# Output projection of a decoder block: six of eight row tiles in pairs with seven block products

## The chip, the cores and the metric

One core of a Trainium2 chip runs the whole kernel. The metric is the device time of one execution in microseconds. Engines are named as in the profile: PE is TensorE, DVE VectorE, ACT ScalarE, POOL GpSimd, SP the engine whose queue issues most DMAs.

## The reference

A hybrid decoder block on x of 1024 tokens by 1024 channels (f32): adaLN-modulated norm, a projection, a gated linear attention branch and a differential attention branch, the gated merge of both, an output projection, and then a mixture of 32 experts of which each token takes two. What the change concerns:

```python
merged = (jax.nn.sigmoid(gate_a) * (o_a @ w_branch_a[l])
          + jax.nn.sigmoid(gate_b) * (o_b @ w_branch_b[l]))
x = x + gate1 * (merged @ w_out[l])
h2 = rms_norm(x, norm2_g[l]) * (1.0 + scale2) + shift2
y = hier_moe(h2, router_group_w[l], router_group_b[l], router_expert_w[l],
             router_expert_b[l], expert_w1[l], expert_w3[l], expert_w2[l])
x = x + gate2 * y
```

## The kernel before, in words

All matmuls are f32; each one of the code appears as two records in the trace. Nearly every matmul is issued through the helper `mm` (line 794), most of VectorE's additions and products through `tt` (line 1946), scalar_tensor_tensor through `stt` (line 1954), and ScalarE's work through `act` (line 1565). Engines are kept in step by counting semaphores, written out by hand; an engine's instructions run in the order in which they stand.

**Merge.** The merged activations are computed transposed into `mT`, 8 channel tiles by 1024 tokens, two channel tiles at a time. This stage already uses a scheme of seven block products for eight (`gate_products` and `branch_products` from line 1243, with VectorE's additions in `gate_adds`, `branch_adds`, `gate_branch_a` and `gate_branch_b`, lines 2441 to 2524). The last merge into `mT` raises `g_free` to 4 + 2 * KT.

**Output projection.** Eight row tiles of 128 tokens. Tile t needs, for each half of 512 output channels, 8 matmuls that accumulate over the channel tiles (`out_proj`, line 1314): stationary is a 128 x 128 piece of the tile that GpSimd has copied from `mT` into `ms` (`stage_merged`, line 687), moving is a piece of w_out of 512 columns. Tile 0 is taken straight from `mT` (lines 1307 to 1312), and its first 6 matmuls are issued ahead of the wait for the last merge. Even tiles write banks 0 and 1, odd tiles banks 2 and 3.

**What follows a tile.** VectorE multiplies each half by gate1 and adds x (`residual`, line 2568); ScalarE squares and sums it and takes the root; VectorE and ScalarE scale half of the row each (`normalised`, `x1_scaled`), and SP stores both forms (`store_x`, line 545). TensorE turns the tile by 8 transposes into banks 4 and 5 (`turn_x1`, line 1323), one VectorE copy (`turned`) and one ScalarE copy evict them, 8 small matmuls form the router's logits transposed (`route_apart`, line 1340), ScalarE reads them and one matmul turns them back (`turn_logits`). VectorE then chooses group and experts in a chain of 17 small dependent steps (`choose`, line 2597). The turning and routing of tile t - 1 is woven into the projection of tile t (`step`, line 1353). In VectorE's queue the order for tile t is: residual of half 0, eviction and choice of tile t - 1, residual of half 1, mean, scaling (lines 2645 to 2670).

**Tile 7.** Its projection is interleaved with the ranks of the tokens of tiles 0 to 5 (`fixed_ranks`, which waits for the choice of tile 5) and the first table of slots (`first_slots`), for which VectorE makes one-hot rows between the residuals (`filled_up`, `first_ids`, `first_onehot`, `first_table`). The last turn, of tile 7, waits for VectorE's last residual. After its routing the expert blocks begin.

**Loads.** SP's queue brings w_out after the last gate product (line 531), then expert weights into ten buffers of 2 MB, of which the buffers in R1, R3, R4, HT and WK come free as the stages end: the tile called (2, 1) behind w_out, (0, 1) and (1, 1) when the merge is done, and (0, 2), (1, 2), (2, 2) behind the stores of tiles 0, 1 and 2; (1, 0) and (0, 0) behind tile 7's two halves (lines 557 to 565). The first expert block uses (0, 1), (0, 2), (1, 1) and (1, 2). From then on each load waits for the block that used its buffer last (lines 582 to 592).

## Time and profile before

| | |
|---|---|
| median of 3 runs | 1479.59 us (1477.48 to 1481.29) |
| profiled execution | 1478.31 us |
| its span | 1476.4 us |
| busy PE / DVE / ACT / POOL | 1430.2 / 629.5 / 334.7 / 110.2 us |
| granted clock, mean | 0.992 |
| output projection | 810 to 940 us of the span |
| expert blocks | from 942 us to the end |

The profile is of one execution, with times from the start of its span. The granted clock is TensorE's, as a share of full speed. A row of a timeline gives start, duration, engine, line, operation, output <- inputs, shape and count of merged instructions; in brackets stands how long the engine was idle ahead of it and what released it. Durations of merged instructions run from the first start to the last end.

### The profile page before, as it was taken

What the parts mean: (1) busy time and instruction counts of PE and PEld (TensorE: products, weight loads), DVE (VectorE), ACT (ScalarE), POOL (GpSimd) and SP (SyncE); (2) the same over time, 40 slices, a digit from 0 to 9 for tenths busy, and PEclk for the clock granted to TensorE, in tenths of its full rate; (3) what the DMA queues carried; (4) which work ended last, traced back from release to release, by engine and by line L of the source; (5) the groups of instructions that cost most, each with busy time, mean ns of one, the idle gap of its engine ahead of it and who ended that gap; (6) DMA issues with size and microseconds to landing.
All of it is one profiled execution on the core that took longest, in us unless ns stands there. A gap on an engine that the chain in (4) does not pass through costs nothing.

```text
span 1476.4 us, 20298 instructions
## 1 busy us (share of the span) xinstructions
PE 1430.2 (97%) x8154; PEld 698.5 (47%) x8154; DVE 629.5 (43%) x1276; ACT 334.7 (23%) x673; POOL 110.2 (7%) x145
## 2 busy tenths in 40 slices
PE   7999999999999999999999999999989899999997
PEld 3544446888886565444444444443323233333332
DVE  4497444747465267554535545752110111111111
ACT  3513322232335453111111222311110111111110
POOL 2000000000000100000000001001121111111111
PEclk9999999999999999999999999999999999999999
DMA  9790200011112101112104752799999999999995
GB/s 357 256 368 1 66 0 1 29 29 29 29 29 58 29 1 43 43 29 57 29 29 171 299 213 85 259 367 404 414 410 409 403 374 394 407 415 404 405 413 168
DMA packets 80285, 292.55 MB, mean 198 GB/s; under 512 B 13408, under 2 KB 42302, under 8 KB 61505
## 3 DMA queue, kind: packets, MB, share of 16 engines
q1 hardware_dynamic: 73634, 274.51, 47.3%
q0 software_dynamic: 6560, 16.77, 4.5%
q8 instruction: 64, 1.05, 0.3%
q14 instruction: 27, 0.22, 0.0%
HBM read 277.47 MB, written 20.09 MB: 202 GB/s over the span
## 4 chain that ended last, share of the span: by engine, by line
PE 86%; DMA 5%; DVE 4%; SPq 3%; issue 1%; ACT 1%; POOL 0%; POOLq 0%; DVEq 0%; ACTq 0%
PE PS L794 81%; DMA R<-in_expert_w 4%; DVE R L1954 3%; SPq L378 2%; PE PS L1387 1%; PE PS L950 1%; PE PS L1470 1%; DMA R<-in_ada_w 0%; PE PS L1328 0%; PE PS L894 0%; DVE R L1946 0%; ACT R L1565 0%; DVE R L1950 0%; SPq L386 0%; PE PS L1162 0%
## 5 line engine op out<-in xcount | busy, mean ns | idle before, releaser
L794 PE MATMUL PS<-R 128*32 128x512 f32 (+4 forms) x3637 | 656.0, 570 | 20.4 <-DMA R<-in_ada_w 9.4
L794 PE MATMUL PS<-HT,R 128*32 128x512 f32 (+1 forms) x1576 | 423.6, 598 | 4.2 <-DMA R<-in_expert_w 4.2
L794 PEld LDWEIGHTS PS<-R 128*32 128x32 f32 (+2 forms) x3637 | 235.3, 127 | 325.8 <-issue 300.1
L794 PEld LDWEIGHTS PS<-HT,R 128*32 128x32 f32 (+1 forms) x1576 | 150.0, 138 | 195.1 <-issue 193.6
L794 PE MATMUL PS<-R,HT 128*128 128x512 f32 (+1 forms) x672 | 235.2, 506 | 2.6 <-ACT R L1565 1.5
L1946 DVE TENSOR_TENSOR R<-R,PS 128x512 f32<-128x512 f32 (+1 forms) x86 | 66.2, 780 | 343.0 <-PE PS L794 342.9
L1565 ACT ACTIVATE R<-PS 128x512 f32<-128x512 f32 (+3 forms) x116 | 69.6, 611 | 463.5 <-PE PS L794 302.4
L794 PEld LDWEIGHTS PS<-R,HT 128*128 128x128 f32 x672 | 125.8, 191 | 93.3 <-issue 82.0
L794 PE MATMUL PS<-WK,R 128*32 128x512 f32 (+1 forms) x440 | 98.0, 606 | 0.0
L1954 DVE SCALAR_TENSOR_TENSOR R<-PS,R,gate 128x1024 f32<-128x1024 f32 (+1 forms) x23 | 28.5, 1238 | 127.4 <-PE PS L794 127.4
L752 POOL DMA_INDIRECT out_rows<-R x36 | 52.3, 1453 | 298.8 <-DVE R L1954 158.5
L1946 DVE TENSOR_TENSOR R<-R 128x256 f32<-128x256 f32 (+11 forms) x109 | 65.7, 625 | 18.2 <-PE PS L794 16.3
L1565 ACT ACTIVATE R<-PS,att_nm 128x128 f32<-128x128 f32 (+7 forms) x64 | 46.8, 736 | 108.8 <-DVE att_nm L1950 108.8
L1565 ACT ACTIVATE R<-PS,S,A 128x128 f32<-128x128 f32 x92 | 34.4, 457 | 156.5 <-PE PS L1387 156.5
L794 PE MATMUL PS<-R,WK 128*128 128x128 f32 (+2 forms) x352 | 63.4, 324 | 2.1 <-DVE R L1950 1.6
L1565 ACT ACTIVATE WK<-PS 128x512 f32<-128x512 f32 (+8 forms) x56 | 34.1, 609 | 115.5 <-PE PS L950 48.7
L794 PEld LDWEIGHTS PS<-R,WK 128*128 128x128 f32 x352 | 46.8, 191 | 16.3 <-issue 16.1
L2165 DVE TENSOR_REDUCE att_mx<-PS 128x2 f32<-128x256 f32 (+7 forms) x32 | 43.3, 1354 | 20.6 <-PE PS L794 20.4
L1565 ACT ACTIVATE WK<-R 128x128 f32<-128x128 f32 (+2 forms) x56 | 34.2, 611 | 77.3 <-DVE R L1946 73.9
L1954 DVE SCALAR_TENSOR_TENSOR R<-R,cact 128x2048 f32<-128x2048 f32 (+1 forms) x23 | 46.6, 2026 | 3.0 <-DMA R<-in_ada_w 1.2
L794 PE MATMUL PS<-R,gate 128*128 128x256 f32 (+1 forms) x224 | 47.1, 366 | 0.0
L794 PEld LDWEIGHTS PS<-R,gate 128*128 128x128 f32 x224 | 39.5, 190 | 6.4 <-issue 1.7
(275 smaller groups left out, 935.2 us busy)
## 6 DMA issues: line engine op xcount, KB each, us to landing
R<-in_expert_w SPq DMA_DIRECT2D x38, 2048.0 KB, 22.9
R<-in_expert_w SPq DMA_DIRECT2D x48, 1024.0 KB, 13.0
HT<-in_expert_w SPq DMA_DIRECT2D x15, 2048.0 KB, 26.9
R<-in_ada_w SPq DMA_DIRECT2D x16, 1024.0 KB, 5.0
HT<-in_expert_w SPq DMA_DIRECT2D x16, 1024.0 KB, 13.2
WK<-in_expert_w SPq DMA_DIRECT2D x7, 2048.0 KB, 25.4
R<-in_w_in SPq DMA_DIRECT2D x24, 512.0 KB, 4.1
R<-in_ada_w SPq DMA_DIRECT2D x16, 512.0 KB, 10.7
```

What stands on the lines that cost most here:

```text
L378: e.dma_start(dst, src, allow_slow_non_contiguous=True).then_inc(s[loaded], 16)
L752: e.indirect_dma_start(out, bass.IndirectOffsetOnAxis(idx, 0), rows_out, None, compute_op=ALU.add, bounds_check=T - 1, oob_is_err=False).t ...
L794: return nc.tensor.matmul(o, l, r, start=a, stop=z)
L950: last = nc.tensor.transpose(bank(4 + j // 4)[:, (j % 4) * P:(j % 4 + 1) * P], attn[i % 2][:, j * P:(j + 1) * P], ident[:, :])
L1387: last = nc.tensor.transpose(bank(j // 4)[:, (j % 4) * P:(j % 4 + 1) * P], xg[u][:, j * P:(j + 1) * P], ident[:, :])
L1470: last = nc.tensor.transpose(bank(4)[:, j * P:(j + 1) * P], hh[:, j * P:(j + 1) * P], ident[:, :])
L1565: return nc.scalar.activation(o, i, f, **kw)
L1946: return v.tensor_tensor(o, a, b, op)
L1954: return v.scalar_tensor_tensor(out=o, in0=a, scalar=c, in1=b, op0=op0, op1=op1)
L2165: att(v.tensor_reduce(att_mx[:, i % 2, :], score_v[:, :, 0:(i + 1) * P], AX.X, ALU.max))
```

## The change

Tiles 0 to 5 are projected as three pairs of 256 tokens. A pair's rows, the 1024 channels in between and the 1024 output channels are each halved, and the two by two blocks are multiplied with seven block products (each four matmuls) instead of eight:

- GpSimd makes sums and differences: of w_out once (`ot1`, `ot2`, `ot4`, 2048 elements a partition each; `ot3` is made by VectorE within the last merge step), and of each pair's activations (`os1` to `os4`, 512 elements each, `pair_sums`). It copies only tiles 6 and 7 as before.
- TensorE runs `pair_steps`: seven products into banks 0, 2, 1, 3, 0, 1, 2. All of it stands behind the wait for the last merge. Between the products of pair q the turning and routing of both tiles of pair q - 1 is placed; that of tiles 4 and 5 goes into tile 6. The logits of odd tiles use bank 7.
- ScalarE copies the first product into SBUF (`pair_first`), VectorE makes seven additions a pair (early, middle, late) with the tiles in `pair_c`, then both tiles' residuals from SBUF (`pair_residual`), then their scaling and evictions. Choices of pair q - 1 stand between the additions of pair q, those of tiles 4 and 5 behind pair 2: tile 4 ahead of the residual of tile 6, tile 5 between its halves.
- Three expert weight tiles that were loaded during the projection are issued behind the pairs, since their buffers now hold the sums.

The diff without waits that only count on and without renamed counts:

```diff
+        ob11, ob12, ob21, ob22 = (wout_h[n][:, k:k + 4, :] for k in (0, 4) for n in range(2))
+        ot1, ot2, ot3, ot4 = (x.rearrange("p (k n) -> p k n", k=4) for x in
+                              (R1[:, 4096:6144], R3[:, 0:2048], R1[:, 6144:8192], R3[:, 3072:5120]))
+        os1, os2, os3, os4 = (R4[:, 6144 + 512 * i:6656 + 512 * i].rearrange("p (k t) -> p k t", k=4) for i in range(4))
+        pair_c = [sig[:, x, :] for x in range(4)]
+        NPAIR = 3
...
-            load_ew(2, 1, FIXED[1])
...
-                if t < 3:
-                    load_ew(t, 2, FIXED[2])
+                if t == 0:
+                    load_ew(2, 2, FIXED[2])
+                if t == 3:
+                    e.wait_ge(s["mo_mm"], 7 * NPAIR)
+                    load_ew(2, 1, FIXED[1])
+                if t == 4:
+                    e.wait_ge(s["x1_ready"], 4 * NPAIR)
+                    load_ew(1, 2, FIXED[2])
+                if t == 5:
+                    e.wait_ge(s["mo_mm"], 7 * NPAIR + 2)
+                    load_ew(0, 2, FIXED[2])
             store_x(NT - 2, 0)
-            e.wait_ge(s["mo_mm"], 2 * NT - 1)
+            e.wait_ge(s["mo_mm"], 7 * NPAIR + 3)
             load_ew(1, 0, FIXED[0])
-            e.wait_ge(s["mo_mm"], 2 * NT)
+            e.wait_ge(s["mo_mm"], 7 * NPAIR + 4)
...
+            def pair_sums(q):
+                a11, a12, a21, a22 = token_pair(q)
+                if q > 0:
+                    e.wait_ge(s["mo_mm"], 7 * q - 5)
+                e.tensor_tensor(os3, a11, a21, ALU.subtract).then_inc(s["st_s"], 1)
+                if q > 0:
+                    e.wait_ge(s["mo_mm"], 7 * q - 3)
+                e.tensor_tensor(os1, a21, a22, ALU.add).then_inc(s["st_s"], 1)
+                e.wait_ge(s["st_s"], 50 + 4 * q)
+                e.tensor_tensor(os2, os1, a11, ALU.subtract).then_inc(s["st_s"], 1)
+                e.wait_ge(s["st_s"], 51 + 4 * q)
+                if q > 0:
+                    e.wait_ge(s["mo_mm"], 7 * q)
+                e.tensor_tensor(os4, a12, os2, ALU.subtract).then_inc(s["st_s"], 1)
+
+            e.wait_ge(s["in_ld9"], 48)
+            e.wait_ge(s["st_t"], 13)
+            e.tensor_tensor(ot1, ob12, ob11, ALU.subtract).then_inc(s["st_t"], 1)
+            e.wait_ge(s["st_t"], 14)
+            e.tensor_tensor(ot2, ob22, ot1, ALU.subtract).then_inc(s["st_t"], 1)
             e.wait_ge(s["g_free"], 4 + 2 * KT)
-            stage_merged(1, 1)
-            with e.Fori(1, NT // 2) as i:
-                for u in range(2):
-                    wait_apart(e, (s["mo_mm"], 2 * (2 * i + u) - 2))
-                    stage_merged(2 * i + u, u)
-
-
-            e.wait_ge(s["ms_ready"], NT - 1)
+            pair_sums(0)
+            e.wait_ge(s["st_t"], 15)
+            e.tensor_tensor(ot4, ob21, ot2, ALU.subtract).then_inc(s["st_t"], 1)
+            stage_merged(NT - 2, 0)
+            for q in range(1, NPAIR):
+                pair_sums(q)
+            e.wait_ge(s["mo_mm"], 7 * NPAIR)
+            stage_merged(NT - 1, 1)
...
-            for half in range(2):
-                for k in range(KT):
-                    if half == 0 and k == KT - 2:
-                        e.wait_ge(s["g_free"], 4 + 2 * KT)
-                    last = mm(bank(half), mT[:, k, 0:P], wout[half][k], k == 0, k == KT - 1)
-                last.then_inc(s["mo_mm"], 1)
+            e.wait_ge(s["g_free"], 4 + 2 * KT)
...
+            def pair_product(b, x, w):
+                for k in range(4):
+                    ins = mm(bank(b), x[:, k, :], w[:, k, :], k == 0, k == 3)
+                ins.then_inc(s["mo_mm"], 1)
...
+            def pair_steps(q):
+                a11, a12, a21, a22 = token_pair(q)
+                added, sums = ADDED_MERGE + 7 * q, 48 + 4 * q
+                if q > 0:
+                    e.wait_ge(s["st_u"], added - 2)
+                pair_product(0, a11, ob11)
+                yield
+                if q > 0:
+                    e.wait_ge(s["st_u"], added)
+                e.wait_ge(s["st_s"], sums + 1)
+                pair_product(2, os3, ot3)
+                yield
+                e.wait_ge(s["st_t"], 15)
+                e.wait_ge(s["st_s"], sums + 3)
+                pair_product(1, os2, ot2)
+                yield
+                pair_product(3, os1, ot1)
+                yield
+                e.wait_ge(s["st_m1"], 13 + q)
+                pair_product(0, a12, ob21)
+                yield
+                e.wait_ge(s["st_t"], 16)
+                e.wait_ge(s["st_u"], added + 1)
+                pair_product(1, a22, ot4)
+                yield
+                e.wait_ge(s["st_s"], sums + 4)
+                e.wait_ge(s["st_u"], added + 2)
+                pair_product(2, os4, ob22)
...
+            def turn_both(t):
+                turn_x1(t, t % 2, 0)
+                turn_x1(t, t % 2, 1)
 
             e.wait_ge(s["small_ld"], 16 * (N_SMALL + 2))
-            with e.Fori(0, NT // 2 - 1) as i:
-                for u in (1, 0):
-                    step(2 * i + 2 - u, u)
-                    out_proj(2 * i + 2 - u, u, 1, 2, 4)
-                    turn_logits(2 * i + 1 - u)
-                    out_proj(2 * i + 2 - u, u, 1, 4, KT)
+            for q in range(NPAIR):
+                product_of_pair = pair_steps(q)
+                next(product_of_pair)
+                if q > 0:
+                    turn_both(2 * q - 2)
+                next(product_of_pair)
+                if q > 0:
+                    turn_both(2 * q - 1)
+                    route_apart(2 * q - 2, 0)
+                next(product_of_pair)
+                if q > 0:
+                    turn_logits(2 * q - 2)
+                    route_apart(2 * q - 1, 1)
+                next(product_of_pair)
+                if q > 0:
+                    turn_logits(2 * q - 1)
+                for _ in range(3):
+                    next(product_of_pair)
+            out_proj(NT - 2, 0, 0, 0, 4)
+            turn_both(NT - 4)
+            out_proj(NT - 2, 0, 0, 4, KT)
+            turn_both(NT - 3)
+            route_apart(NT - 4, 0)
+            out_proj(NT - 2, 0, 1, 0, 4)
+            turn_logits(NT - 4)
+            route_apart(NT - 3, 1)
+            out_proj(NT - 2, 0, 1, 4, KT)
+            turn_logits(NT - 3)
...
+            def pair_first(q):
+                e.wait_ge(s["mo_mm"], 7 * q + 1)
+                e.wait_ge(s["g_free"], 4 + 2 * KT)
+                e.wait_ge(s["x1_ready"], 4 * q)
+                act(pair_c[0], bank(0), ACT.Copy).then_inc(s["st_m1"], 1)
+
+            pair_first(0)
+            for q in range(NPAIR):
+                for u in range(2):
+                    t = 2 * q + u
+                    for half in range(2):
+                        x1_square(t, u, half)
+                    x1_root(t, u)
+                    if u == 0:
+                        x1_turned(t, u)
+                x1_scaled(2 * q, 0)
+                x1_turned(2 * q + 1, 1)
+                x1_scaled(2 * q + 1, 1)
+                if q + 1 < NPAIR:
+                    pair_first(q + 1)
+                logits_read(2 * q)
+                logits_read(2 * q + 1)
...
+                if p == KT // 2 - 2:
+                    e.wait_ge(s["in_ld9"], 48)
+                    tt(ot3, ob22, ob12, ALU.subtract).then_inc(s["st_t"], 1)
...
+            def pair_adds_early(q):
+                c11, c12, c21, c22 = pair_c
+                added = ADDED_MERGE + 7 * q
+                e.wait_ge(s["st_m1"], 13 + q)
+                e.wait_ge(s["mo_mm"], 7 * q + 3)
+                e.wait_ge(s["x1_ready"], 4 * q)
+                tt(c12, c11, bank(1), ALU.add).then_inc(s["st_u"], 1)
+                e.wait_ge(s["st_u"], added + 1)
+                tt(c21, c12, bank(2), ALU.add).then_inc(s["st_u"], 1)
+
+            def pair_adds_middle(q):
+                c11, c12, c21, c22 = pair_c
+                added = ADDED_MERGE + 7 * q
+                e.wait_ge(s["st_u"], added + 2)
+                e.wait_ge(s["mo_mm"], 7 * q + 4)
+                tt(c22, c21, bank(3), ALU.add).then_inc(s["st_u"], 1)
+                tt(c12, c12, bank(3), ALU.add).then_inc(s["st_u"], 1)
+
+            def pair_adds_late(q):
+                c11, c12, c21, c22 = pair_c
+                added = ADDED_MERGE + 7 * q
+                e.wait_ge(s["mo_mm"], 7 * q + 5)
+                tt(c11, c11, bank(0), ALU.add).then_inc(s["st_u"], 1)
+                e.wait_ge(s["st_u"], added + 4)
+                e.wait_ge(s["mo_mm"], 7 * q + 6)
+                tt(c21, c21, bank(1), ALU.add).then_inc(s["st_u"], 1)
+                e.wait_ge(s["mo_mm"], 7 * q + 7)
+                tt(c12, c12, bank(2), ALU.add).then_inc(s["st_u"], 1)
+                e.wait_ge(s["st_u"], added + 7)
+
+            def pair_residual(q, u):
+                t = 2 * q + u
+                for half in range(2):
+                    x, c = slice(half * 512, (half + 1) * 512), pair_c[2 * u + half]
+                    if half == 0:
+                        e.wait_ge(xn_st[u], 16 * (t // 2 + 1))
+                        e.wait_ge(s["mods_ld"], 16 * 6)
+                    tt(c, c, gate[:, 0, x], ALU.mult).then_inc(s["mo_gated"], 1)
+                    e.wait_ge(s["mo_gated"], 2 * t + half + 5)
+                    e.wait_ge(xh_ld[u], 16 * (t // 2 + 1))
+                    tt(xh[u][:, x], xh[u][:, x], c, ALU.add).then_inc(s["x1_ready"], 1)
+                mean_square(t)
...
+            def tail_begin(q):
+                pair_residual(q, 0)
+                pair_residual(q, 1)
+                normalised(2 * q)
+                turned(2 * q)
+                e.wait_ge(s["xn2_ready"], 4 * q + 2)
+                normalised(2 * q + 1)
+                turned(2 * q + 1)
+
+            pair_adds_early(0)
+            pair_adds_middle(0)
+            pair_adds_late(0)
+            for q in range(1, NPAIR):
+                tail_begin(q - 1)
+                if q == 1:
+                    rt(v.memset(prior_b[:, 0, :], 0.0))
+                pair_adds_early(q)
+                choose(2 * q - 2)
+                pair_adds_middle(q)
+                choose(2 * q - 1)
+                pair_adds_late(q)
+            tail_begin(NPAIR - 1)
+            choose(NT - 4)
+
+            for t in (NT - 2, NT - 1):
...
```

## Rows read from the trace of the kernel before

**Rows 1.** The chain that ended last, from the page: shares of the span by engine.

```profile
PE 86%; DMA 5%; DVE 4%; SPq 3%; issue 1%; ACT 1%; POOL 0%; POOLq 0%; DVEq 0%; ACTq 0%
```

**Rows 2.** Stretches of 6 us: PE, PEld, DVE, ACT, POOL busy, granted clock, DMA share, GB/s.

```profile
804.00:810.00 6.00, 6.00 (x15) 2.65 (x14) 3.48 (x6) 0.00 (x0) 0.00 (x0) 1.00 0.00 1
...
924.00:930.00 6.00, 6.00 (x27) 3.34 (x28) 4.73 (x14) 2.45 (x4) 0.00 (x0) 1.00 0.54 178
...
964.00:970.00 6.00, 6.00 (x60) 1.82 (x56) 5.31 (x21) 0.60 (x1) 0.00 (x0) 1.00 0.58 199
...
976.00:982.00 6.00, 4.80 (x44) 3.60 (x48) 4.56 (x10) 1.50 (x4) 0.00 (x0) 1.00 1.01 421
```

**Rows 3.** Timeline of PE in the expert stage: the longest waits for weights.

```profile
1107.29 1.07 PE L794 MATMUL PS<-R 128*32 128x512 f32 x2 [3.95 <-DMA WK<-in_expert_w]
...
1112.38 0.69 PE L794 MATMUL PS<-R 128*32 128x512 f32 x2
...
1170.03 0.63 PE L794 MATMUL PS<-HT,R 128*32 128x512 f32 x3 [4.17 <-DMA R<-in_expert_w]
```

**Rows 4.** Timeline of PE in the output projection: turns of tiles and the last turn.

```profile
810.25 20.80 PE L794 MATMUL PS<-HT,R 128*128 128x512 f32 x48
...
830.88 1.04 PE L1328 MATMUL PS<-ident,R 128*128 128x128 f32 x8
...
846.92 1.04 PE L1328 MATMUL PS<-ident,R 128*128 128x128 f32 x8
...
847.79 1.88 PE L794 MATMUL PS<-HT,R 128*128 128x512 f32 x4
...
911.05 1.04 PE L1328 MATMUL PS<-ident,R 128*128 128x128 f32 x8
...
939.29 0.66 PE L1328 MATMUL PS<-ident,R 128*128 128x128 f32 x4 [0.38 <-DVE R L1946]
...
941.81 3.62 PE L794 MATMUL PS<-R 128*32 128x512 f32 x16
```

**Rows 5.** Timeline of DVE, tiles 5 to 7: sixth choice, residuals, its one wait.

```profile
916.91 0.25 DVE L1954 SCALAR_TENSOR_TENSOR small_w<-PS,stat,rbias 128x36 f32<-128x36 f32 x1 [3.64 <-PE PS L794]
...
921.18 0.69 DVE L1946 TENSOR_TENSOR WK<-PS,gate 128x512 f32<-128x512 f32 x1
...
922.51 0.15 DVE L1951 TENSOR_SCALAR stat<-stat 128x1 f32<-128x1 f32 x1
...
927.87 0.69 DVE L1946 TENSOR_TENSOR WK<-PS,gate 128x512 f32<-128x512 f32 x1 [0.94 <-PE PS L794]
```

**Rows 6.** Timeline of DVE at the end of the merge.

```profile
800.11 0.69 DVE L1946 TENSOR_TENSOR R<-R,WK 128x512 f32<-128x512 f32 x1
...
809.52 0.69 DVE L1946 TENSOR_TENSOR gate<-gate,WK 128x512 f32<-128x512 f32 x1
...
814.59 0.69 DVE L1946 TENSOR_TENSOR R<-R 128x512 f32<-128x512 f32 x1
```

**Rows 7.** Instructions by line and form: GpSimd's and VectorE's elementwise rows.

```profile
L644 POOL TENSOR_TENSOR tri<-tri,blk 64x128 f32<-64x128 f32 x1 | 0.4, 447 | 0.1
...
L683 POOL COPY WK<-R 128x512 f32 x4 | 2.5, 613 | 34.9 <-PE PS L794 34.9
...
L688 POOL COPY R<-R 128x1024 f32 x6 | 6.3, 1045 | 83.0 <-PE PS L794 83.0
...
L1946 DVE TENSOR_TENSOR R<-R 128x1024 f32<-128x1024 f32 x20 | 24.2, 1222 | 16.5 <-PE PS L794 16.3
```

**Rows 8.** Timelines: a small VectorE addition beside a GpSimd copy, and alone.

```profile
840.44 1.04 POOL L688 COPY R<-R 128x1024 f32 x1 [14.97 <-PE PS L794]
...
840.48 1.02 DVE L1946 TENSOR_TENSOR R<-R 128x32 bf16<-128x32 bf16 x1
...
904.54 0.17 DVE L1946 TENSOR_TENSOR R<-R 128x32 bf16<-128x32 bf16 x1
```

**Rows 9.** Stretch of 2 us behind the last wait for weights, columns as in rows 2.

```profile
1172.00:1174.00 2.00, 2.00 (x16) 0.78 (x12) 0.00 (x0) 0.00 (x0) 0.00 (x0) 0.51 0.97 363
```

More of the change, by code:

```diff
@@ L331, in build, with mean_no, root_no @@
         wout = [[w[:, k, :] for k in range(KT)] for w in wout_h]
+        ob11, ob12, ob21, ob22 = (wout_h[n][:, k:k + 4, :] for k in (0, 4) for n in range(2))
[4 more added lines that the diff above has]
+        NPAIR = 3
+        def mean_no(t):
+            return 2 * t + 1 - (t % 2 if t < 2 * NPAIR else 0)
+        def root_no(t):
+            return 2 * t + 2 + (1 - t % 2 if t < 2 * NPAIR else 0)
+        ADDED_MERGE = 28 * (KT // 2 - 1)
+        ADDED_PAIRS = ADDED_MERGE + 7 * NPAIR
         xh = [R4[:, 4096 + 1024 * i:5120 + 1024 * i] for i in range(2)]
-        ms = [R4[:, 6144 + 1024 * i:7168 + 1024 * i].rearrange("p (k t) -> p k t", k=KT) for i in range(2)]
+        ms = [x.rearrange("p (k t) -> p k t", k=KT) for x in (R3[:, 2048:3072], R4[:, 6144:7168])]
         xn = [WK[:, 1024 * i:1024 * (i + 1)] for i in range(2)]
@@ L1316, in out_proj @@
                     if half == 0:
-                        e.wait_ge(s["ms_ready"], t)
-                    e.wait_ge(s["mo_gated"], 2 * t + half + 1)
+                        e.wait_ge(s["ms_ready"], u + 1)
+                    e.wait_ge(s["st_u"], ADDED_PAIRS - 2 + half if u == 0 else ADDED_PAIRS)
                 for k in range(k0, k1):
@@ L1340, in route_apart @@
             def route_apart(t, u):
-                e.wait_ge(s["rt_done"], t + 1)
+                e.wait_ge(s["rt_done"], max(t, 1))
                 for k in (0, 4, 1, 5, 2, 6, 3, 7):
@@ L1345, in route_apart @@
                     r = 64 * (k // 4)
-                    last = mm(bank(6)[r:r + NR, 64:64 + P], wr[:, k, :], h2T[u][:, k, :], k % 4 == 0, k % 4 == 3)
+                    last = mm(bank(6 + u)[r:r + NR, 64:64 + P], wr[:, k, :], h2T[u][:, k, :], k % 4 == 0, k % 4 == 3)
                 last.then_inc(s["rt_pr"], 1)
@@ L1869, in logits_read @@
                 for r in (0, 64):
-                    last = act(logits_t[r:r + NR, :], bank(6)[r:r + NR, 64:64 + P], ACT.Copy)
+                    last = act(logits_t[r:r + NR, :], bank(6 + t % 2)[r:r + NR, 64:64 + P], ACT.Copy)
                 last.then_inc(s["rt_lg"], 1)
-            for half in range(2):
-                x1_square(0, 0, half)
-            x1_norm(0, 0)
-            with e.Fori(0, NT // 2 - 1) as i:
-                for u in (1, 0):
-                    t = 2 * i + 2 - u
-                    x1_turned(t - 1, 1 - u)
-                    x1_square(t, u, 0)
-                    logits_read(t - 1)
-                    x1_square(t, u, 1)
-                    x1_norm(t, u)
+            def pair_first(q):
[19 more added lines that the diff above has]
+                logits_read(2 * q + 1)
+            for half in range(2):
+                x1_square(NT - 2, 0, half)
+            x1_norm(NT - 2, 0)
             x1_turned(NT - 2, 0)
@@ L2570, in residual @@
                 c = slice(half * 512, (half + 1) * 512)
-                e.wait_ge(s["mo_mm"], 2 * t + half + 1)
+                e.wait_ge(s["mo_mm"], 7 * NPAIR + 2 * (t - NT + 2) + half + 1)
                 if half == 0:
@@ L2600, in choose @@
                 c = slice(t, t + 1)
-                stt(logits[:, t, :], bank(6)[:, 0:NR], stat[:, 2, t % 2:t % 2 + 1], rbias[:, :], ALU.mult, ALU.add).then_inc(s["rt_done"], 1)
+                stt(logits[:, t, :], bank(6 + t % 2 if t < 2 * NPAIR else 6)[:, 0:NR], stat[:, 2, t % 2:t % 2 + 1], rbias[:, :], ALU.mult, ALU.add).then_inc(s["rt_done"], 1)
                 e.wait_ge(s["rt_done"], t + 2)
@@ L2643, in first_table @@
                 stt(tab_tok[:, c], pad, -1.0, a, ALU.add, ALU.add).then_inc(s["tab_done"], 1)
-            for t in range(NT):
+            def tail_begin(q):
[21 more added lines that the diff above has]
+            for t in (NT - 2, NT - 1):
                 if t == NT - 1:
```

39 lines of the change are left out of this document (18 added, 21 removed).

## The prediction

> **What bounds the kernel now.** I read the page's chain of waits first [rows 1]. The reader is to see that TensorE holds 86% of the chain that ends last and VectorE 4%. Then I read the stretches of 6 us. From 976 us on the transfers run at 421 GB/s with the 16 DMA engines full [rows 2], and TensorE stands for weights there, the longest times for 3.95 and 4.17 us [rows 3]. Every load of that stretch waits for a buffer that TensorE has finished with, and from 964 to 970 us, ahead of the saturation, the transfers still have room (0.58 busy, [rows 2]) because no buffer is free. So the expert stage hangs on the moment at which TensorE enters it. I take a shift of that entry to reach the end one for one.
>
> In the stage that is changed, TensorE has no gap: the last branch product gives way to row tile 0 at 810.25, and the turns of tiles come every 16.03 us (831 and 847, [rows 4]). VectorE waits for TensorE in every tile. That holds up to the last tile: from the start of the sixth choice at 916.91 to the last residual VectorE stands only 0.94 us [rows 5], and TensorE waits for that residual at 939.29 [rows 4]. The entry at 941.8 thus follows the end of VectorE's queue.
>
> **What is saved.** From 810.25 to 830.88 TensorE works off 48 records [rows 4], 0.43 us each; two records are one matmul, 0.858 us, so a product of four takes 3.43. A pair needs 28 of them where two tiles needed 32: 3.43 us less, 10.3 us for three pairs.
>
> **The start.** Before, 6 matmuls (5.15 us) of tile 0 run ahead of the last merge, which ends at 815.28 [rows 6]. Afterwards TensorE waits for that merge with nothing to do, from 810.25. That cover of 5.0 us is lost whatever else happens.
>
> VectorE gets one subtraction of 2048 elements a partition. No row has this form; 1024 elements take 1.22 us [rows 7] and 512 take 0.69 [rows 6], so 2.3 us, from 800.75 to 803.05. Between there and 809.52 stand six branch additions of 0.69 that wait for TensorE's products, 1.72 us apart, so 2.3 us of the wait are used up and the queue catches up. I cost it at nothing. The transfers are idle from 804 [rows 2], with an expert tile of 5 us behind w_out, so w_out is there by 799; without this cover up to 2.3 us would fall on the merge.
>
> GpSimd then makes the first two weight differences, 2048 elements each, ahead of the merge. The one tensor_tensor it has is 447 ns for 128 elements [rows 7]. Copies of 512 and 1024 take 0.61 and 1.045 us, about 0.2 us and 0.84 ns an element. With that fixed part the tensor_tensor costs 2.1 ns an element: 4.5 us for 2048, 1.25 us for 512. The lower bound is the copy's rate, 1.9 us for 2048; the upper is a smaller fixed part, 4.8 us. I take 4.5, since that row is the same operation. They run 803.1 to 807.6 and 807.6 to 812.1.
>
> VectorE's products and merges from 809.52 on read SBUF twice. The rows show what that means: an addition of 32 columns takes 0.17 us alone and 1.02 us when it meets a GpSimd copy, and both end together, at 841.5 [rows 8]. So the operation of 809.52 starts at 812.1: 2.6 us. The Trainium skill (SBUF — State Buffer, Who interferes with whom) says that such a VectorE instruction and a GpSimd one that reads SBUF exclude each other for a whole instruction. By that rule the long differences block as I charge them; if a hold were never longer than the copies show, the start would cost 1.6 us less. The bounds of this term are 0 (differences at the copy's rate, over by 807) and 3.2 us. The merge ends at 817.9, and TensorE has been idle for 7.7 us.
>
> After idle times of 3.95 and 4.17 us the granted clock fell to 0.5 (0.51 from 1172 to 1174), the lower level of 1.2 GHz, and matmuls of 0.6 us took 1.07 [rows 3, 9]. It was low from 1107.3 to about 1112.4 and from about 1170.5 to 1173.8, and half of that is lost: 2.6 and 1.7 us. I take 2.1 us for the restart; the bounds are 0 and, for the longer idle time, twice the smaller, 3.4.
>
> Pair 0 has no turns between its products: 817.9 + 24.0 + 2.1 = **844.0** for its end. GpSimd's four sums (5 us) and the last difference (4.5 us) end 9.7 us into it; its products need them from 3.4 and from 17 us on, so they cost nothing. Were my rate for them half as much again, they would still be in time.
>
> **Pairs 1 and 2.** A tile's routing work costs 16.03 - 13.73 = 2.3 us of TensorE, 4.6 a pair. New are waits at each border between pairs. After a pair's last product VectorE has one addition left (0.69) and then eight operations of 0.69 at 0.60 to 0.72 apart, where before it had two after a half tile. GpSimd's fourth sum is released at the same instant and blocks the first of them until 1.6 us after the border. The second half of tile 2q is ready 4.35 us after it; TensorE, with one product and four turns, is there at 3.87. Half a microsecond. The first tile's eviction from the shared turn bank stands behind the second tile's residual, at 9.2 us; TensorE asks at 8.7. Another half. Bounds 0 and 3 us a pair; I take 1.1. A pair thus lasts 24.0 + 4.6 + 1.1 = 29.7 us. Additions, choices and late additions of VectorE fit in it: the choice takes 4.3 us undisturbed [rows 5] and the sums on GpSimd add 1 to 2 us. Pair 2 ends at 844.0 + 59.4 = **903.4**. Before, tile 6 starts at 911.05 - 6.87 = 904.2 [rows 4]. TensorE is level.
>
> **The tail.** At this point the old order had one tile left to turn and route; the new one has two, and their choices stand one behind the other in VectorE's queue with one half's residual between. Before, the sixth choice starts 12.7 us after tile 6 (916.91). Now the fifth starts there, plus one turn (0.87, [rows 4]) and the border's 1.1: 14.7 us. It takes 4.3, the residual 1.3 (921.18 to 922.51, [rows 5]), and the sixth choice starts at 903.4 + 20.3 = 923.7. From there the queue is the old one, less the 0.94 us that it stood: 923.7 - 916.9 - 0.9 = **5.9 us later**. TensorE waits for it at the ranks, the first slots and the last turn. The bounds here: 0 if the choices were hidden by TensorE, 2 us more if GpSimd's constants block them.
>
> **The loads.** Three expert tiles (2 MB, some 5 us each at 400 GB/s) leave SP's queue at 788, 835 and 848 us and come behind the pairs; the fourth moves from the third tile's store to the first's. Behind the pairs the engines are 0.54 busy or less, as from 924 to 930 [rows 2]; 6 MB fit, and they are issued by 922, more than 20 us ahead of the first block. The queue entries behind them (x of tiles 6 and 7) are needed over 8 us after they can land. Nothing, with 3 us as the upper bound.
>
> **Sum.** Up to the end of pair 2: -10.3 (products) + 5.0 (cover) + 2.6 (blocked VectorE) + 2.1 (clock) + 2.2 (two borders) = +1.6 us, and one routing of 2.3 us fewer has been done by then than at the start of tile 6 before: -0.7, which is the 903.4 against 904.2. The tail then adds 6.7: **+5.9 us**. The profiled execution took 1478.31 us (span 1476.4), which gives 1484.2; the median of the runs stands 1.3 us above it, and I give **1485.5**.
>
> **Rivals.**
> 1. *VectorE's tail is hidden* (not slower). Then TensorE's own count decides: tile 6 with two routings and a border takes 13.7 + 4.6 + 1.1 = 19.4 us, and tile 7 starts at 922.8 where it started at 904.2 + 16.0 = 920.2: +2.6 us, 1482, within what can be told. For it speaks that VectorE waits in each tile now; against it that its queue is already full behind tile 5. It decides if the sixth choice starts by 920.4, 2.6 us after its old time and the 0.9 us of standing. Chance 0.17.
> 2. *The start is cheap*: differences at the copy's rate, no block, and a restart at full clock. 4.7 us less, +1.2: 1481. Chance 0.12.
> 3. *The weight stream takes up the delay*: if the loads didn't move with TensorE, the 8.1 us of the two waits and 4.3 us of low clock [rows 3] would shrink, and the end would come at 1472 to 1480. Against it: the engines are not full before 970 us. Chance 0.11.
> 4. *VectorE and GpSimd block each other in every choice*, also in the tail: 3 us a pair, 2 us behind, 1490 to 1494. Chance 0.10.
> That the products don't fall to seven is excluded by the code. My forecast has 0.50.
>
> **Numbers.** A measurement tells 0.3% (4.4 us) from no change. Faster by more needs rival 3 nearly whole: 0.08. Within 0.3%: rivals 1 and 2, part of 3, and the lower third of my own case: 0.40. Slower: 0.52. The range runs from rival 2 and the upper part of 3 to the lower end of rival 4: 1478.5 to 1491.
>
> **What would show it.** TensorE idle 7 to 8 us ahead of the first pair product, with two GpSimd tensor_tensor of 4.5 us and a VectorE product ending late beside the second; a stretch at 0.5 behind it; borders with two waits of half a microsecond; the end of pair 2 at 903; the sixth choice at 923.7; the last turn at 945. It is wrong if TensorE reaches that turn without a wait, if GpSimd takes 2 us, or if the weight waits shrink.

## The result and the profile after

The changed kernel takes 1486.03 us (median of 5 runs, 1485.38 to 1487.08), the kernel before 1479.59 (5 runs): a ratio of 1.0047, 95% interval 1.0036 to 1.0059. It is slower by 0.5%, and 1485.5 had been predicted.

The profiled execution took 1487.06 us, its span is 1485.2. Already a GpSimd fill at 492.25 us stands 2.59 us later than before (489.66), where the two programs are the same. I take this shift, and its like in every trace below, off and call what is left local. The start times in the rows are as the profile has them. The last turn came at 939.29 [rows 4] and comes at 948.36: 9.07 later, 6.5 us local. The spans differ by 8.8 - 2.6 = 6.2.

TensorE around pair 0 of the changed kernel (timeline: start, duration, engine, line, operation, count, idle time ahead and its releaser):

```profile
802.54 10.46 PE L841 MATMUL PS<-R 128*128 128x512 f32 x24
820.72 5.61 PE L841 MATMUL PS<-HT,R 128*128 128x512 f32 x8 [7.71 <-DVE R L2060]
826.16 10.46 PE L841 MATMUL PS<-R 128*128 128x512 f32 x24
836.47 3.60 PE L841 MATMUL PS<-HT,R 128*128 128x512 f32 x8
839.90 3.60 PE L841 MATMUL PS<-R 128*128 128x512 f32 x8
843.33 7.03 PE L841 MATMUL PS<-HT,R 128*128 128x512 f32 x16
850.20 0.60 PE L1408 MATMUL PS<-ident,R 128*128 128x128 f32 x4
```

Before, this engine had no gap here [rows 4]. The first product behind the gap takes 5.61 us where a later one takes 3.60; the granted clock is 0.50 from 820 to 824 us and 1.00 from 826 us on. The 16 records at 843.33 are pair 0's last product and pair 1's first, so pair 0 ends at 846.77. GpSimd and VectorE meanwhile (two timelines, of POOL and of DVE):

```profile
805.75 4.52 POOL L733 TENSOR_TENSOR R<-HT 128x2048 f32<-128x2048 f32 x1 [251.01 <-DVE R L2060]
810.35 4.50 POOL L735 TENSOR_TENSOR R<-HT,R 128x2048 f32<-128x2048 f32 x1
...
820.54 1.27 POOL L720 TENSOR_TENSOR R<-R 128x512 f32<-128x512 f32 x1 [5.68 <-DVE R L2060]
```

```profile
811.39 0.69 DVE L2060 TENSOR_TENSOR WK<-WK,PS 128x512 f32<-128x512 f32 x1 [1.10 <-PE PS L841]
812.12 3.28 DVE L2060 TENSOR_TENSOR gate<-gate,WK 128x512 f32<-128x512 f32 x1
815.33 0.68 DVE L2060 TENSOR_TENSOR R<-R,WK 128x512 f32<-128x512 f32 x1
...
819.77 0.69 DVE L2060 TENSOR_TENSOR R<-R 128x512 f32<-128x512 f32 x1
```

The product at 812.12 takes 3.28 us where its like take 0.69. It lies beside the second difference and ends at 815.40, just behind the end of that one at 814.85. The last merge, at 819.77, is 2.6 us late for it. The tail of the stage, TensorE first, then GpSimd, then VectorE:

```profile
908.94 1.25 PE L1408 MATMUL PS<-ident,R 128*128 128x128 f32 x8
915.34 0.63 PE L1408 MATMUL PS<-ident,R 128*128 128x128 f32 x4 [1.28 <-DVE WK L2742]
930.23 0.55 PE L841 MATMUL PS<-R 128*128 128x24 bf16 x6 [1.20 <-DVEq L2774]
936.35 0.31 PE L841 MATMUL PS<-R 128*128 128x2 bf16 x6 [1.06 <-DVE R L2060]
947.45 1.06 PE L1487 MATMUL PS<-ident,R 128*128 128x128 f32 x8 [1.59 <-DVE WK L2060]
948.36 0.60 PE L1408 MATMUL PS<-ident,R 128*128 128x128 f32 x4
```

```profile
939.90 2.02 POOL L784 DMA_INDIRECT R<-xn_rows,R  x1 [25.69 <-DMA xn_rows<-WK]
```

```profile
938.32 0.55 DVE L2068 SCALAR_TENSOR_TENSOR R<-R 128x1 f32<-128x1 f32 x3
```

TensorE stands four times, 5.1 us, where it stood 0.4 [rows 4]. The last of these stands is ahead of the transposes of the gathered rows (L1487), which the first expert block needs. The indirect DMA that fetches those rows (the gather) starts at 939.90. The bracket of its row names a store, but the gather waits only for the stores of tiles 0 to 5, of which the last, issued at 917.37, landed 12.0 us later, and for VectorE's first table, which is done at 938.87. The gather starts 1.0 us behind the table, as it did before (930.54 and 931.53). TensorE takes up its rows at 947.45, 7.5 us behind its start; before, it had landed after 5.5 us.

Behind the entry, the waits for weights did not shrink, which settles the rival of the stream that takes up a delay (summary of TensorE's waits from 960 us on: total, times, longest; after, then before):

```profile
PE PS L841 <- DMA R<-in_expert_w: 8.8, 3, 4.1
PE PS L841 <- DMA WK<-in_expert_w: 4.0, 1, 4.0
```

```profile
PE PS L794 <- DMA R<-in_expert_w: 7.8, 3, 4.2
PE PS L794 <- DMA WK<-in_expert_w: 4.0, 1, 4.0
```

### The profile page after: what moved, and what is told of

It is laid out like the page before. It is cut to its first block and busy times, and to the rows that moved or that the text cites. A ratio compares the mean times of both kernels' runs of the same rounds, so it can differ in the third digit from the quotient of the medians.

```text
span 1485.2 us, 20233 instructions
## 1 busy us (share of the span) xinstructions
PE 1423.6 (96%) x8130; PEld 696.1 (47%) x8130; DVE 651.4 (44%) x1298; ACT 334.4 (23%) x676; POOL 136.5 (9%) x155
## 5 line engine op out<-in xcount | busy, mean ns | idle before, releaser
L841 PE MATMUL PS<-R 128*32 128x512 f32 (+5 forms) x3733 | 697.0, 568 | 24.7 <-DMA R<-in_ada_w 9.6
L841 PEld LDWEIGHTS PS<-R 128*32 128x32 f32 (+3 forms) x3733 | 252.5, 128 | 349.0 <-issue 318.4
L841 PE MATMUL PS<-HT,R 128*32 128x512 f32 (+1 forms) x1456 | 373.0, 601 | 11.9 <-DVE R L2060 7.7
L2060 DVE TENSOR_TENSOR R<-R,PS 128x512 f32<-128x512 f32 x107 | 80.2, 762 | 366.4 <-PE PS L841 362.7
L841 PEld LDWEIGHTS PS<-HT,R 128*32 128x32 f32 (+1 forms) x1456 | 128.8, 135 | 181.6 <-issue 180.7
L2060 DVE TENSOR_TENSOR R<-R 128x512 f32<-128x512 f32 (+11 forms) x121 | 73.2, 625 | 18.6 <-PE PS L841 16.3
## 6 DMA issues: line engine op xcount, KB each, us to landing
R<-in_expert_w SPq DMA_DIRECT2D x48, 1024.0 KB, 12.5
```

What stands on the lines that cost most here:

```text
L841: return nc.tensor.matmul(o, l, r, start=a, stop=z)
L2060: return v.tensor_tensor(o, a, b, op)
```

## Experiments

The measured ratios are to runs of the kernel before on the same chip. In us a ratio is multiplied by its 1480. The changed kernel was not run again beside them; its 1.0047 is that of the result. Each interval reaches 1.3 to 2.2 us to either side, so a step of 1 or 2 us rests on its one trace.

**Start, cover alone: the kernel before, with TensorE's tile 0 behind the last merge.**

```diff
             e.wait_ge(s["g_sig"], 4 * (KT - 2))
+            e.wait_ge(s["g_free"], 4 + 2 * KT)
             for half in range(2):
```

> The kernel before, with one wait added: TensorE's row tile 0 stands until the last merge, as the pairs do. Nothing else is changed. Theory (the cover is worth 5.0 us and the shift reaches the end one for one, with about 1.5 us more of low clock behind an idle time of 5 us): every turn of a row tile comes 5.0 to 7.0 us later, the entry to the experts too, the end at 1479.6 + 6.5 = 1486. Rival 1 (the weight stream takes up the delay): entry 6 us later, end less than 2 us later, the waits for weights shorter. Rival 2 (VectorE's queue of the last tiles has slack that swallows it): entry less than 3 us later.

Measured: 1486.87 us, ratio 1.0046 (1.0032 to 1.0061), 6.8 us. TensorE's timeline, and the two stretches behind the wait (PE, PEld, DVE, ACT, POOL busy, granted clock, DMA share, GB/s):

```profile
818.22 22.91 PE L794 MATMUL PS<-HT,R 128*128 128x512 f32 x48 [5.01 <-DVE R L1947]
...
949.37 0.66 PE L1329 MATMUL PS<-ident,R 128*128 128x128 f32 x4 [0.37 <-DVE R L1947]
```

```profile
818.00:822.00 4.00, 3.78 (x5) 1.74 (x6) 1.35 (x4) 0.00 (x0) 1.04 (x1) 0.50 0.71 208
822.00:826.00 4.00, 4.00 (x10) 1.68 (x10) 0.61 (x4) 0.00 (x0) 0.00 (x0) 0.95 1.04 398
```

The 48 records took 20.80 us [rows 4] and take 22.91, 2.1 us more, at a clock of 0.50 at first. With the 5.01 us of idle time this is 7.1, and the last turn comes 10.08 - 2.79 = 7.3 us late (local), with the same wait ahead of it. Cover and restart (the low clock behind an idle time) together reach the end one for one. Both rivals fall.

**Start, block alone: GpSimd's second difference behind the merge.**

```diff
-            e.wait_ge(s["st_t"], 14)
-            e.tensor_tensor(ot2, ob22, ot1, ALU.subtract).then_inc(s["st_t"], 1)
...
                 e.tensor_tensor(os3, a11, a21, ALU.subtract).then_inc(s["st_s"], 1)
+                if q == 0:
+                    e.wait_ge(s["st_t"], 14)
+                    e.tensor_tensor(ot2, ob22, ot1, ALU.subtract).then_inc(s["st_t"], 1)
```

> The changed kernel with GpSimd's second weight difference (4.5 us) placed behind the last merge and the first sum instead of ahead of it, where it lay beside a VectorE product that ended 2.6 us late. Theory (VectorE and GpSimd hold each other off): that product takes 0.69 us instead of 3.28, the last merge ends 2.6 us earlier and pair 0 starts 2.6 us earlier; the idle time is 5.1 us. The three sums behind the difference come 4.5 us later, but 6 us into a pair of 24, with the products that need them from 3.4 to 17 us on: up to 2 us of wait at the third or fourth product. Time 1483.4 without that wait, 1485.4 with it. Rival (VectorE's product ended late because TensorE's products or ScalarE's reads came late, and the difference only lay beside it): the merge ends where it did, 1486 or later.

Measured: 1483.04 us, ratio 1.0021 (1.0011 to 1.0030). The same product on VectorE, then TensorE's first product:

```profile
808.99 0.69 DVE L2061 TENSOR_TENSOR gate<-gate,WK 128x512 f32<-128x512 f32 x1
```

```profile
814.99 5.12 PE L842 MATMUL PS<-HT,R 128*128 128x512 f32 x8 [5.12 <-DVE R L2061]
```

Without the difference beside it the product takes 0.69 us and TensorE's idle time falls by 2.59. No later product of pair 0 waits. The last turn comes 3.2 us earlier than in the changed kernel (local). The difference beside the product was the cause of its length.

**Start, clock alone: 8 idle matmuls.**

```diff
             e.wait_ge(s["g_sig"], 4 * (KT - 2))
+            for _ in range(8):
+                mm(bank(5), ident[:, :], wout[0][0])
             e.wait_ge(s["g_free"], 4 + 2 * KT)
```

> The changed kernel with 8 more matmuls of 128 x 128 by 512, whose result nobody reads, in TensorE's 7.7 us of idle time ahead of pair 0. Nothing starts earlier; only the idle time is filled. Theory (the restart at the low clock costs 2.0 us): no stretch at 0.50 behind the wait, the second and third pair products at 0.43 us a record from their start, pair 0 ends 2.0 us earlier, 1484.0, a ratio of 1.0033. Rival (the low stretch costs nothing that reaches the end, because GpSimd's sums or VectorE would hold pair 0 anyway): pair 0 ends where it did, 1486.

Measured: 1484.37 us, ratio 1.0024 (1.0015 to 1.0033). TensorE:

```profile
812.94 7.03 PE L841 MATMUL PS<-HT,ident 128*128 128x512 f32 x16
820.62 3.70 PE L841 MATMUL PS<-HT,R 128*128 128x512 f32 x8 [0.65 <-DVE R L2062]
```

The first product takes 3.70 us and not 5.61, the granted clock stays at 1.00, and pair 0 ends 2.1 us earlier (local), of which 0.2 us are an earlier start. The last turn gains 1.6: half a us is lost again at the gathered rows, where TensorE now stands 2.1 us. The runs differ from the changed kernel's by more, 3.4 us; the trace does not show the rest.

**Start, products moved ahead of the merge.** The first product of pair 0, then the first two with GpSimd's sum for the second. The cut below is TensorE's part of the second edit; GpSimd's waits ahead of its sums move in the same way. In the first edit the second product keeps the wait for the merge.

```diff
-            e.wait_ge(s["g_free"], 4 + 2 * KT)
+            e.wait_ge(s["g_free"], 2 * KT)
...
+                if q == 0:
+                    e.wait_ge(s["g_free"], 4 + 2 * KT)
```

> The changed kernel, with the first pair product of pair 0 let ahead of the wait for the last merge: it reads only channel tiles 0 to 3, which are there. Theory (the loss is the cover of the last merge, each us of TensorE's start reaches the end one for one): TensorE's 7.7 us of idle time become 4.3, the end comes 3.4 us earlier than in the changed kernel, 1482.6 on the scale of its median of 1486.0, a ratio of 1.0023 to the kernel before instead of 1.0047. The low clock behind the wait stays, since 4.3 us are about as long as the waits of 3.95 and 4.17 us that it followed before. Rival 1 (the end hangs on VectorE's queue of the last tiles, not on TensorE's start): the start moves by 3.4 us and the last turn by less than 1. Rival 2 (the clock's restart is tied to the long idle time): it goes too, 5.4 us earlier, 1480.6.

> The changed kernel, with the first two pair products of pair 0 ahead of the wait for the last merge, and GpSimd's sum for the second of them made as soon as its channel tiles are there. Theory: 6.9 us of the 7.7 us of idle time are filled, the granted clock doesn't fall, so 6.9 + 2.0 = 8.9 us less than the changed kernel: 1477.1, a ratio of 0.9985 to the kernel before. GpSimd's sum of 1.26 us ahead of ot1 may push its queue and VectorE's last merge back by up to 1.3 us: 1478.4 at worst. Rival 1 (VectorE's queue of the last tiles sets the end): less than 2 us gained, 1484 or more. Rival 2 (the clock costs nothing): 1479.

Measured: 1483.46 us, ratio 1.0017 (1.0008 to 1.0027), and 1483.26, 1.0019 (1.0010 to 1.0027). The first comes out near its time, but with 5.51 us of idle time where 4.3 were expected, and its last turn is only 2.3 us earlier (local). The second was a miss. TensorE in the two:

```profile
822.21 12.13 PE L841 MATMUL PS<-R 128*128 128x512 f32 x24 [5.51 <-POOL R L720]
```

```profile
823.68 8.80 PE L845 MATMUL PS<-R 128*128 128x512 f32 x16 [4.02 <-POOL R L729]
```

Each product moved ahead brings the next one to GpSimd's sums, of which two, 1.26 us each, can only follow the last merge. In my sum they cost nothing; that held only while a product without sums stood ahead of them. The clock fell behind the idle 4.02 us too (0.53 from 826 to 828 us).

**Loads alone, in the kernel before: first with the waits of the changed kernel.**

```diff
-            load_ew(2, 1, FIXED[1])
...
-                if t < 3:
-                    load_ew(t, 2, FIXED[2])
+                if t == 0:
+                    load_ew(2, 2, FIXED[2])
+                if t == 3:
+                    e.wait_ge(s["mo_mm"], 12)
+                    load_ew(2, 1, FIXED[1])
+                if t == 4:
+                    e.wait_ge(s["x1_ready"], 12)
+                    load_ew(1, 2, FIXED[2])
+                if t == 5:
+                    e.wait_ge(s["mo_mm"], 14)
+                    load_ew(0, 2, FIXED[2])
```

> The kernel before, with three loads of expert weights (2 MB each) moved behind the row tiles 5 and 6, where the changed kernel has them. Theory: nothing, 1479.6 within 1 us, the waits for weights of 3.95 and 4.17 us and the entry at 941.8 as they were. Rival (the later loads push the weight stream back, and part of the changed kernel's loss is theirs): up to 3 us later, with longer waits for weights from 1100 us on.

Measured: 1487.01 us, ratio 1.0046 (1.0034 to 1.0058). This does not tell what the loads cost. TensorE stands in a new place, for VectorE, which waits for a store:

```profile
921.03 1.92 PE L802 MATMUL PS<-WK,wr 128*36 128x128 f32 x14 [5.33 <-DVE WK L2590]
```

```profile
917.58 0.69 DVE L1954 TENSOR_TENSOR WK<-PS,gate 128x512 f32<-128x512 f32 x1 [6.72 <-DMA xn_rows<-WK]
```

My wait for the end of tile 5, put behind x of tile 5, held the store of tile 4 in SP's queue (at 906.78 us where it stood at 891.10 before). In the changed kernel SP stands 12.5 us for the same event, but there the next store is due only at 909.50 us. So once more, with no wait added:

```diff
-            load_ew(2, 1, FIXED[1])
...
-                if t < 3:
-                    load_ew(t, 2, FIXED[2])
+                if t == 0:
+                    load_ew(2, 2, FIXED[2])
+                if t == 5:
+                    load_ew(2, 1, FIXED[1])
+                    load_ew(1, 2, FIXED[2])
             store_x(NT - 2, 0)
+            load_ew(0, 2, FIXED[2])
```

> The kernel before, with the same three loads of expert weights (2 MB each) moved back, but without a wait of their own: two stand behind the request for x of tile 7 (some 912 us), one behind the stores of tile 6 (some 925 us). In the experiment before, they stood behind waits that also held the stores of tiles 4 and 5 and the request for x of tile 6; its 7.8 us may be those waits' and not the loads'. Theory: the loads cost nothing, 1479.3 within 1.5 us, a ratio of 1.000, the entry to the experts where it was, no wait of TensorE ahead of tile 6. Rival (the loads themselves cost: they keep the transfers of x and the stores of tiles 6 and 7 back, or the weights of the experts): 3 to 8 us more, with the last residuals waiting for transfers.

Measured: 1482.96 us, ratio 1.0029 (1.0014 to 1.0043). TensorE at the gathered rows; then loads, stores and the gather among the issues between 925 and 950 us (KB each, us to landing), first in this kernel, where no landing of the gather is recorded, then in the one before:

```profile
943.68 1.06 PE L1390 MATMUL PS<-ident,R 128*128 128x128 f32 x8 [2.21 <-issue]
```

```profile
HT<-in_expert_w SPq DMA_DIRECT2D x4, 1024.0 KB, 10.3
xn_rows<-WK SPq DMA_DIRECT2D x2, 512.0 KB, 6.1
```

```profile
HT<-in_expert_w SPq DMA_DIRECT2D x4, 1024.0 KB, 6.1
xn_rows<-WK SPq DMA_DIRECT2D x2, 512.0 KB, 4.9
R<-xn_rows,R POOLq DMA_INDIRECT x1, 5.5
```

From 925 to 950 us packets take 99% of the DMA engines' time, before 78%. The gather starts where it did (934.98 - 3.43 = 931.55, before 931.53), so no store holds it. It is not there when TensorE asks at 941.47: its rows are used 8.7 us behind its start, where it had landed after 5.5. The last turn comes 5.29 - 3.43 = 1.9 us late (local). The runs give 4.3 us, with an interval from 2.1; what lies above 1.9 the trace does not show.

**Tail: two pairs in place of three.**

```diff
-        NPAIR = 3
+        NPAIR = 2
```

(and tiles 5 and 6 taken back into the old order on all engines)

> The changed kernel with two pairs in place of three: row tiles 0 to 3 in pairs, 4 to 7 in the old way. Theory (the third pair saves 3.43 us, but makes VectorE's queue of the last tiles 6.7 us late, and with tiles 5 to 7 one by one VectorE catches up before tile 7): 6.7 - 3.43 - 1.1 for a border, with up to 1 us of the tail left: 2.5 to 4.4 us less than the changed kernel, 1482 to 1483.5, a ratio of 1.002. VectorE stands in tile 6 again, and the last residual is waited for by less than 1 us. Rival (the tail isn't late because of the third pair; the loss is all at the start): 3.4 us more than the changed kernel less a border of 1, 1488.

Measured: 1485.84 us, ratio 1.0043 (1.0031 to 1.0055), the last turn 0.2 us earlier (local). A miss, and of arithmetic: TensorE's own work is longer by 3.43 us, which the sum had left out, and of the 5.1 us of waits 1.7 stay. The third pair saves what it costs.

> Two pairs in place of three, and the first two products of pair 0 ahead of the wait for the last merge. Theory (the two losses are apart and add): 8.9 + 3.5 us less than the changed kernel, 1473.6, a ratio of 0.996 to the kernel before, faster than both. Rival (one slack is shared, so that after the first gain the second is worth nothing): 1477.

The edit is the two before, together. Measured: 1482.23 us, ratio 1.0019 (1.0010 to 1.0029), as with three pairs. Neither the theory nor the rival had it, since both counted on the 8.9 us at the start.

**The start filled.** The first two products run ahead of the merge as above. VectorE makes the two sums that follow the merge, GpSimd the second difference behind it, and the product that reads it comes fifth. VectorE's part:

```diff
+            e.wait_ge(s["g_free"], 4 + 2 * KT)
+            tt(os1, v21, v22, ALU.add).then_inc(s["st_s"], 1)
+            e.wait_ge(s["st_s"], 50)
+            tt(os2, os1, v11, ALU.subtract).then_inc(s["st_s"], 1)
```

> The changed kernel with all of TensorE's 7.7 us of idle time filled: the first two products of pair 0 run ahead of the wait for the last merge; VectorE makes the two sums that need the last merge (0.7 us each in place of 1.26 on GpSimd, behind each other); GpSimd makes the second weight difference behind the merge, and the product that reads it comes fifth in pair 0 and not third. The moved first two products alone gave 3.6 us and not 8.9, because TensorE then stood 4.0 us for GpSimd's sums and the clock still fell. Theory: TensorE stands for less than 1 us ahead of pair 0's third product, the granted clock stays at 1.00, the entry to the experts comes 9 us earlier than in the changed kernel: 1477, a ratio of 0.998 to the kernel before. Rival (VectorE's queue or GpSimd's differences of 4.5 us now hold a later product of pair 0): 2 to 4 us of it come back, 1480.

> The same with two pairs in place of three. Two pairs alone gave 0.2 us in the trace, because TensorE's own count is 3.43 us longer and only the 5 us of waits on VectorE in the last tiles go. Theory (the third pair saves what it costs, whatever the start): the same as with three pairs within 1 us, 1477. Rival (with the start filled, the end of VectorE's queue matters more, and two pairs win): 2 to 3 us less than with three.

Measured: 1478.27 us, ratio 0.9991 (0.9980 to 1.0002), and with two pairs 1478.06, 0.9991 (0.9982 to 1.0001). The gap ahead of pair 0 is gone, and inside the pair 3.7 us have come back, as the rival had it: 1.93 of a wait and 1.8 of low clock. GpSimd, VectorE and TensorE of the version with three pairs:

```profile
825.77 4.51 POOL L743 TENSOR_TENSOR R<-HT,R 128x2048 f32<-128x2048 f32 x1
```

```profile
826.50 4.79 DVE L2700 COPY suf<-ident 36x36 f32<-36x36 f32 x2
831.33 3.33 DVE L2072 TENSOR_TENSOR R<-R,PS 128x512 f32<-128x512 f32 x5
```

```profile
832.16 5.37 PE L845 MATMUL PS<-R 128*128 128x512 f32 x8 [1.93 <-DVE R L2072]
```

The two small copies of 36 columns stand beside the difference for 4.79 us, the additions stand behind it, and TensorE behind them; the product takes 5.37 us and not 3.6, at a low clock again (0.57 from 832 to 834 us). With two pairs the wait is there too, 1.92 us, but the clock stays at 1.00.

**The last two differences on VectorE too** (two pairs).

```diff
+            e.wait_ge(s["st_t"], 14)
+            tt(ot2, ob22, ot1, ALU.subtract).then_inc(s["st_t"], 1)
+            e.wait_ge(s["st_t"], 15)
+            tt(ot4, ob21, ot2, ALU.subtract).then_inc(s["st_t"], 1)
```

> Two pairs, the start filled as in the runs before, and GpSimd's last two weight differences (2048 elements each) made by VectorE instead, right behind the last merge. In the trace of the run before, GpSimd's last difference held a VectorE copy for 4.8 us, VectorE's first additions of the pair stood behind it, and TensorE stood 1.9 us for them in the middle of pair 0. Theory: VectorE makes both differences in 4.6 us while nothing else is due on it, TensorE has no wait over 0.7 us in pair 0 and the clock stays at 1.00: 1.9 us less than with GpSimd, 1476.5, a ratio of 0.998 to the kernel before, an interval that leaves 1 out. Rival (VectorE's additions now stand behind its own differences, or the stream of expert weights takes up the gain): 1478, as before.

Measured: 1477.07 us, ratio 0.9981 (0.9972 to 0.9990): faster than the kernel before by 0.2%, and than the changed one. Against the version with GpSimd's differences (0.9982 to 1.0001) the intervals overlap; in the traces the last turn is 0.9 us earlier (local). VectorE and TensorE:

```profile
819.69 5.56 DVE L2086 TENSOR_TENSOR R<-HT,R 128x2048 f32<-128x2048 f32 x2
```

```profile
830.77 3.67 PE L840 MATMUL PS<-R 128*128 128x512 f32 x8 [1.04 <-DVE R L2086]
937.41 1.06 PE L1506 MATMUL PS<-ident,R 128*128 128x128 f32 x8 [0.23 <-issue]
938.33 0.66 PE L1418 MATMUL PS<-ident,R 128*128 128x128 f32 x4
```

Two differences take 5.56 us here, and the clock stays at 1.00 from 812 to 836 us. One wait of 1.04 us was left in the pair where I had expected 0.7 at most. The last turn is 2.9 us earlier than in the kernel before (local), where two pairs take 6.9 us of work off TensorE: 3.1 us are its waits in this trace, and about 1 us is not placed.

## Why the prediction was right, and where not

The last turn was put at some 945 us and came at 945.8 (local). The entry to the experts was put 5.9 us later and came 950.82 - 2.59 - 941.81 = 6.4 later. By its steps (all times local):

| Step | predicted | measured |
|---|---|---|
| idle time ahead of pair 0 | 7.7 | 7.71 |
| GpSimd's first two differences | 4.5 each | 4.52, 4.50 |
| GpSimd's first sum | 1.25 | 1.27 |
| blocked VectorE product, added | 2.6 | 2.59 |
| low clock behind the idle time | 2.1 | 2.05 |
| VectorE's own difference | 2.3 | 2.28 |
| end of pair 0 | 844.0 | 844.2 |
| pairs 1 and 2 | 29.7 each | 29.77, 28.97 |
| end of pair 2 | 903.4 | 902.9 |
| sixth choice | 923.7 | 923.68 |
| end of VectorE's last residual, later by | 5.9 | 5.6 |
| moved loads, at the last turn | 0 | 0.9 |

- *Start.* Each of its terms was also changed alone. The cover of 5.0 us and its low clock, added to the kernel before, cost 7.3 us; moving the difference gave 2.59 back; the idle matmuls took 1.9 of the 2.05 us of low clock out. VectorE's difference cost nothing: TensorE's last branch product ended within 0.2 us of where it did. The rival of a cheap start is out at each point. The Trainium skill (SBUF — State Buffer, Who interferes with whom) has a VectorE instruction with two inputs in SBUF and a GpSimd one that reads SBUF exclude each other for a whole instruction, and the trace agrees: the product waited for the end of the 4.5 us difference.
- *Pairs.* The first border has its two waits, 0.20 and 0.61 us, the second only one of 0.20. Pairs of 29.8 us and less leave nothing of the rival of blocks in every choice.
- *Tail.* The rival of a hidden tail wanted the sixth choice by 920.4, and it came at 923.68. From there the queue is the old one. TensorE waits at the ranks and the first slots as predicted, but not at the last turn, which I had named as a sign of being wrong. It stood 1.59 us just ahead of it, at the gathered rows, and VectorE's last residual ended at 947.37, 0.08 us before the rows were used. So the tail hangs on VectorE as predicted, and on the gather beside it.
- *Loads at nothing.* This term was mis-sized. "They fit, and are issued by 922, more than 20 us ahead of the first block" looked at their own deadline, not at who shares the DMA engines and the queue. With the loads beside it the last store of tile 5 took 12.0 us to land (2.6 before). The request for x of tile 7 stood in SP's queue until 928.12 for the store before it, and the last load behind that request until 928.49. The gather took 7.5 us and not 5.5, and its rows hold TensorE 1.59 us. With the rows in time, their 0.9 us of transposes would have been done before VectorE's last residual ended; so 0.9 us is what the loads add here, an estimate from the rows. In the kernel before, where VectorE is early, they cost 1.9 us in the trace and 4.3 in the runs.
- *Not in the sum:* GpSimd's constants. VectorE's scaling of tile 4 took 2.26 us beside a fill of 1.80 us, in place of 0.8, and is a part of the first wait of 1.28. I had kept this as a bound. That the fill is the cause is read from the trace; no experiment moved it.

The time was met to 0.5 us in part by luck: pair 2 ended 0.5 us early and VectorE was 0.3 us quicker behind the sixth choice, against 0.5 us lost ahead of that choice and 0.9 for the loads.

That the change is slower comes from the start: 5.0 + 2.6 + 2.1 us, against products worth 10.3, of which the third pair's 3.4 are eaten by VectorE's queue. With the start filled the ratio falls from 1.0047 to 0.9991.

What the runs leave open: the load experiment's 2.4 us beyond its trace, and some 2 us between trace and runs also with the idle matmuls, with one product moved and with the start filled (three pairs). The shifts ahead of the stage (-0.5 to 3.4 us between profiles) have no explanation here, and single traces can be compared only after they are taken off.

## What to carry over

Where a saving needs prepared operands, cost the first use by itself: what ran ahead of the producer's last step before, and which of the new operands can only follow that step. Give the preparation of long operands to the engine whose queue is empty just then, since the engine on the path can be held for the rest of the other's instruction (2.6 us here). A load moved to where the DMA engines look half empty is to be checked against the small transfers there, here a store and a gather, and not against its own deadline alone.

## What the hardware showed that was not expected

- Two VectorE copies of 36 columns took 4.79 us beside a GpSimd difference, and 0.37 where GpSimd was quiet. A block's price is what stands behind it: nothing in the changed kernel, where the two took 4.74 us, and 1.9 us and a clock drop in the filled one.
- The blocking goes both ways: with both differences on VectorE, GpSimd's sum took 3.25 us in place of 1.26, and the two differences 5.56 us in place of 2 x 2.3.
- The granted clock fell behind idle times of 4.0, 5.0, 5.1, 5.5 and 7.7 us. Behind 1.93 us it fell in one trace (5.37 us for the product) and not in that of the version with two pairs, behind 1.92 (3.67 us).
